# Gate sigmoid, early weight splits and table preloads in the mixing phases of a two-layer kernel

## The chip, the cores and the metric

The kernel runs on one core of a Trainium2 chip. The metric is the device time of one launch in microseconds. TensorE has two clock levels, 1.2 and 2.4 GHz; the profile gives the granted clock as a share of the higher.

## What is computed

Two layers over 1024 prompt rows and 32 sample rows of width 1024, everything in float32. Layer 0 has differential attention, layer 1 stick-breaking attention; both end in an output projection, and behind each stands the same mixing step:

```python
x = x + attention(rmsnorm(x), ...) @ w_out
x = x + sigmoid(x @ ple_w_gate[i]) * (p[i] @ ple_w_proj[i])     # p has 256 columns
# after the last layer
y = rmsnorm(x, final_norm_g)
```

Keys and values of both layers are outputs too. The attention's input projection `rmsnorm(x) @ w_in` has 4096 columns, in 8 groups of 512 (q, k, v: 384, gate: 128).

## The kernel before, in words

Each product of float32 data is made of three matmuls on split operands: a value is rounded to a high part (ACT, a Copy), the rest is the low part (DVE, a subtraction), and the helper `three` at line 107 issues high x high, low x high and high x low. So each matrix is split before it is used, weights too.

The phases stand one behind the other: `lift_phase`, `diff_layer` (names `la_`), `mix_phase` as `mix_a`, `stick_layer` (`lb_`), and `mix_phase` again as `mix_b` with `final_gain`, which makes it the last phase. At the end of a phase all engines meet at a barrier. Each engine has its own program in order, and semaphores tie them; there is no other scheduler.

A mixing phase works feature-major: 8 blocks of 128 output features, and columns (rows of x) in three pieces of 384, 384 and 288. `VISITS` is the order of the work. Visits 0 to 7 are the output projection, one block each. Visits 8 to 15 are gate visits. In `mix_a` each has three units, one a piece. In `mix_b` they have two units (pieces 0 and 1), and visits 16 to 23 go over the blocks again in the reverse order for piece 2, one unit each; there the blocks' weights are loaded and split anew except for the first two. A unit of the gate has 30 matmuls: 6 for p and 24 for x1.

Behind a gate unit stands this chain: DVE bounds the sum (`clamp`, L2049), ACT does Exp (L1930) and Ln with bias 1 (L1932), DVE takes a maximum (`soft`, L2053), ACT does Exp (L1937), DVE multiplies with the p part (`product`, L2058), POOL adds x (`whole` L2113, `add` L2118). In `mix_a` ACT then squares the result (L1948) for the next norm and writes the high part of the next attention's input (L1952), DVE the low part (L2063), POOL sums the squares (L2127), and SP stores the result (L1858) from three buffers, each of which `whole` waits for. TensorE waits for the product of unit v-2 before it starts unit v, since it has two pairs of banks.

The split of the next visit's weights (ACT L1914 and L1916, DVE L2023 and L2025) stands at the head of a visit on both engines, ahead of that visit's units. SP loads a block two visits before its split, once the block's stage half is free.

In `mix_b`'s visits 17 to 22 TensorE also turns a finished tile of 128 rows (`turn`, L2202), ACT forms its statistics (`statistics`: Square L1963, Ln L1967, Exp L1970), DVE scales it (`normed`, L2070) and SP stores it (L1863). The last three tiles come after visit 23.

At the end of `mix_a` ACT and DVE split four of eight blocks of the next attention's first weights (L1999, L2100), TensorE sums the squares over features by a matmul with a constant matrix `mean` (L2226), and once more per token by 18 small matmuls (L2228), and ACT forms the factors of the norm (L2004 to L2010). The token factors are read nowhere later. `stick_layer` then loads and splits blocks 4 to 7 itself (L1119, L1198, L1353), and both halves of the gate's weights (L1202, L1358), while TensorE runs `project` of slots 0 to 5; behind slot 0 it waits for `gw_low` (L1734).

ACT's functions need a table; `preload_act_table_set` names one. It stands in `lift_phase` (L180) for Exp and Ln, and in `stick_layer` (L1324) for Sigmoid. Other table loads are put in by the compiler.

## Time and profile before

| | us |
|---|---|
| median of 3 runs | 1958.19 |
| lowest and highest | 1954.84, 1958.61 |
| the profiled execution | 1955.77 |
| its span, first to last instruction | 1954.0 |
| TensorE busy | 1780.0 (91%) |
| VectorE (DVE) busy | 1023.8 (52%) |
| ScalarE (ACT) busy | 976.7 (50%) |
| GpSimd (POOL) busy | 548.1 (28%) |
| granted clock, mean | 0.972 |

Busy times are shares of one span and overlap each other. `mix_a` runs from about 700 to 959 us, `lb` from 961 to about 1656, `mix_b` to 1954.

### The profile page before, as it was taken

The page shows a single profiled execution, that of the slowest core. Times are in us where ns is not written, and L with a number is a line of the kernel's source. Part 1 is how long each engine was busy: PE and PEld are TensorE (multiplying, and loading weights), DVE is VectorE, ACT ScalarE, POOL GpSimd, SP SyncE. Part 2 cuts the span into 40 slices and gives each one's busy share as a digit, 9 for nine tenths or more (in the row PEclk, how much of TensorE's full clock was granted, in tenths as well). Part 3 has the DMA queues.
Part 4 walks back from the last instruction along what each step waited for, and adds up shares of the span by engine and source line. Part 5 has one row for each costly group of instructions (what it writes and reads, how often), then busy time and mean ns, then how long its engine had stood idle before and what let it go on. Part 6 is the DMA issues. An engine that isn't in the chain of part 4 may idle for free. (4 is left out here: it accounts for less than half of the span.)

```text
span 1954.0 us, 30493 instructions
## 1 busy us (share of the span) xinstructions
PE 1780.0 (91%) x11333; PEld 1580.5 (81%) x11333; DVE 1023.8 (52%) x1821; ACT 976.7 (50%) x2200; POOL 548.1 (28%) x709
## 2 busy tenths in 40 slices
PE   4999999999999989999699999999999997998863
PEld 3878878888788779998598888888888885998863
DVE  5456464564655652256446657565575656434332
ACT  5355454554545542255435445454454545236787
POOL 0131331322313100046314334343343434003310
PEclk9999999999999989999799999999999998999987
DMA  4121111211112043221210212112121122421121
GB/s 155 38 76 47 54 50 40 81 41 54 50 43 81 26 145 98 66 74 52 88 45 23 77 39 61 53 35 77 39 61 42 47 84 73 133 80 44 38 86 57
DMA packets 161507, 124.86 MB, mean 64 GB/s; under 512 B 10960, under 2 KB 152336, under 8 KB 161360
## 3 DMA queue, kind: packets, MB, share of 16 engines
q1 hardware_dynamic: 160496, 122.72, 20.5%
q8 instruction: 91, 1.49, 0.3%
q14 instruction: 56, 0.46, 0.1%
q10 hardware_dynamic: 864, 0.20, 0.0%
HBM read 89.36 MB, written 33.52 MB: 63 GB/s over the span
## 5 line engine op out<-in xcount | busy, mean ns | idle before, releaser
L107 PE MATMUL pj<-h_high,area 128*128 128x384 f32 (+1 forms) x1536 | 380.9, 334 | 17.3 <-issue 5.5
L1517 POOL TENSOR_TENSOR lb_a<-lb_a,lb_remain 128x127 f32<-128x127 f32 (+3 forms) x192 | 237.2, 1255 | 375.1 <-DVE lb_remain L1389 258.6
L107 PE MATMUL pj<-area,h_high 128*128 128x384 f32 (+1 forms) x1152 | 332.1, 351 | 6.7 <-issue 5.5
L107 PEld LDWEIGHTS pj<-h_high,area 128*128 128x128 f32 x1536 | 265.9, 191 | 20.0 <-issue 10.3
L107 PE MATMUL pj<-h_low,area 128*128 128x384 f32 (+1 forms) x768 | 250.5, 326 | 0.0
L1389 DVE TENSOR_TENSOR_SCAN lb_remain<-lb_remain 128x512 f32<-128x512 f32 (+4 forms) x200 | 198.7, 1032 | 67.6 <-ACT lb_remain L1230 66.8
L1230 ACT ACTIVATE lb_remain<-lb_sc 128x512 f32<-128x512 f32 (+4 forms) x200 | 100.1, 501 | 264.5 <-PE lb_sc L1598 234.1
L107 PEld LDWEIGHTS pj<-area,h_high 128*128 128x128 f32 (+1 forms) x1152 | 203.0, 181 | 19.4 <-issue 5.6
L107 PE MATMUL pj<-area,h_low 128*128 128x384 f32 (+1 forms) x576 | 194.7, 338 | 0.0
L107 PEld LDWEIGHTS pj<-h_low,area 128*128 128x128 f32 x768 | 146.3, 191 | 0.0
L455 ACT ACTIVATE la_p<-la_sc,la_nm 128x128 f32<-128x128 f32 (+5 forms) x144 | 105.7, 737 | 33.8 <-DVE la_nm L652 32.9
L757 POOL TENSOR_TENSOR la_ra<-la_tok,cos 128x64 f32<-128x64 f32 (+1 forms) x72 | 23.0, 319 | 335.9 <-ACT la_tok L438 335.9
L1624 PE MATMUL lb_flip<-ident,lb_a 128*128 128x128 f32 (+1 forms) x616 | 94.0, 284 | 22.6 <-POOL lb_a L1517 22.6
L650 DVE TENSOR_REDUCE la_mx<-la_sc 128x1 f32<-128x128 f32 (+5 forms) x144 | 107.6, 747 | 2.2
L107 PEld LDWEIGHTS pj<-area,h_low 128*128 128x128 f32 (+1 forms) x576 | 104.5, 181 | 3.1
L1624 PEld LDWEIGHTS lb_flip<-ident,lb_a 128*128 128x128 f32 (+1 forms) x616 | 64.8, 142 | 50.2 <-POOL lb_a L1517 36.6
L1235 ACT ACTIVATE lb_a<-lb_sc 128x512 f32<-128x512 f32 (+4 forms) x200 | 100.7, 503 | 0.0
L107 PE MATMUL mix_b_g<-mix_b_x_high,area 128*128 128x384 f32 (+1 forms) x384 | 100.5, 349 | 0.0
L1249 ACT ACTIVATE lb_wt<-lb_flip 128x128 f32<-128x128 f32 (+3 forms) x192 | 87.2, 519 | 23.6 <-PE lb_flip L1624 23.6
L107 PE MATMUL mix_a_g<-mix_a_x_high,area 128*128 128x384 f32 (+1 forms) x384 | 91.3, 323 | 0.0
L773 POOL TENSOR_TENSOR area<-stage,area 128x384 fp32r<-128x384 f32 x56 | 64.6, 1181 | 76.1 <-ACT area L427 76.1
L473 ACT ACTIVATE la_wt<-la_third 128x512 f32<-128x512 f32 (+2 forms) x96 | 46.9, 488 | 75.1 <-PE la_third L868 46.5
(305 smaller groups left out, 3988.7 us busy)
## 6 DMA issues: line engine op xcount, KB each, us to landing
stage<-in_a_w_in SPq DMA_DIRECT2D x60, 192.0 KB, 3.3
stage<-in_b_w_in SPq DMA_DIRECT2D x60, 192.0 KB, 3.2
stage<-in_ple_w_gate SPq DMA_DIRECT2D x22, 512.0 KB, 3.7
h_low<-o_t SPq DMA_DIRECT2D x14, 528.0 KB, 6.3
mix_b_xs<-x_mid SPq DMA_DIRECT2D x8, 528.0 KB
lift_xt<-in_x SPq DMA_DIRECT2D x8, 512.0 KB, 4.6
stage<-in_a_w_in SPq DMA_DIRECT2D x16, 256.0 KB, 5.1
out_ak<-la_tok SPq DMA_DIRECT2D x8, 512.0 KB, 3.3
```

The lines of the kernel that those rows point to most:

```text
L107: last = pe.matmul(out, x, y, start=start and n == 0, stop=stop and n == 2, **kw)
L455: act.activation(p[c][u % (3 - c)][0:n, 0:nk], scores_of(u)[:, c, :], ACT.Exp, bias=nm[0:n, u % 2, c:c + 1], accum_out=sums[0:n, u % 2, c: ...
L473: ins = act.activation(wt[:, k0:k0 + nb, off:off + n], bank, ACT.Copy)
L650: dve.reduce_max(mx[0:n, u % 2, c:c + 1], x[:, c, :], AX.X).then_inc(S["dve_link"], 1)
L757: pool.tensor_tensor(xc, x[:, :, 0:16], cos[0:n, t], ALU.mult)
L773: pool.tensor_tensor(w[1][:, k, :], raw_w(k), w[0][:, k, :].bitcast(F32), ALU.subtract).then_inc(S["w_low"], 1)
L1230: act.activation(remain_of(s), scores_of(s), ACT.Sigmoid, scale=-1.0).then_inc(S["keep"], 1)
L1235: act.activation(weights_of(s), scores_of(s), ACT.Sigmoid).then_inc(S["sig"], 1)
L1249: act.activation(wt[hd][:, 4 * c:4 * c + nb, q % 2 * P:(q % 2 + 1) * P], flip[:, hd, 0:width(i)].rearrange("p (b n) -> p b n", n=P), ACT.C ...
L1389: dve.tensor_tensor_scan(out=x, data0=x, data1=x, initial=first, op0=ALU.mult, op1=ALU.min).then_inc(S["scan"], 1)
L1517: pool.tensor_tensor(out, out, after, ALU.mult).then_inc(S["a"], 1)
L1624: last = pe.transpose(flip[0:rows, hd, b // P * n:(b // P + 1) * n], x[:, b:b + rows], ident[0:n, 0:n])
```

## The change

In gate visits below `SECOND` (16), which is all of `mix_a` and the first pass of `mix_b`, the chain is one Sigmoid on ACT and the product. The old chain stays for `mix_b`'s second pass; there the split of the next weights moves between Ln and Exp (ACT) and behind the product (DVE), one visit earlier. Table preloads stand at the start of each mixing phase, at visit 16 of `mix_b`, and ahead of `mix_a`'s last Ln. `mix_a` splits all eight blocks of the next weights: the first four ahead of the last unit's Sigmoid (ACT) and product (DVE), the others behind the last unit, each loaded when a quarter of the stage is free. `stick_layer` no longer loads or splits them, nor waits for `gw_low` behind slot 0. The norm per token goes; `mean` gets memory of its own.

```diff
--- before.py
+++ after.py
@@ -1133,8 +1133,6 @@
...
             load_past(0, Count(table, 0).before("pv"))
-            for k in range(STAGES, KT):
-                load_w(0, k)
             load_gate(0, 1)
@@ -1190,7 +1188,7 @@
...
         def _(act):
-            act.sem_inc(S["w_high"], STAGES)
+            act.sem_inc(S["w_high"], KT)
             start_credits(act, {x: s for x, s in S.items() if x != "w_low"}, 1, 5)
@@ -1317,8 +1315,6 @@
...
 
-            for k in range(STAGES, KT):
-                split_w(0, k)
             for half_ in range(2):
@@ -1332,11 +1328,11 @@
...
         def _(dve):
-            dve.sem_inc(S["w_low"], STAGES + CREDIT)
+            dve.sem_inc(S["w_low"], KT + CREDIT)
             start_credits(dve, {x: s for x, s in S.items() if x != "w_low"}, 2, 5)
...
 
-                dve.sem_inc(S[f"w_loaded{s}"], 16)
+                dve.sem_inc(S[f"w_loaded{s}"], 32)
 
@@ -1488,8 +1484,6 @@
...
 
-            for k in range(STAGES, KT):
-                split_w(0, k)
             for half_ in range(2):
@@ -1730,14 +1724,12 @@
...
                 project(first, x, 1)
-                if x == 0:
-                    pe.wait_ge(S["gw_low"], first.all("gw_low"))
             pe.wait_ge(S["fill"], 1 + 1)
...
 
-def mix_phase(nc, top, name, h, h_offset, stage, area, area_offset, pj, x_in, x_out, p_in, w_out, w_gate, w_proj, ident, norm=None, staged=(),
+def mix_phase(nc, top, name, h, h_offset, stage, area, area_offset, pj, x_in, x_out, p_in, w_out, w_gate, w_proj, ident, norm=None, staged=(), w_next=None,
               final_gain=None):
@@ -1770,6 +1762,9 @@
...
     P_AT = {2 * t + 2: t for t in range(NT + 1)}
+    SECOND = 2 * KT
+    early_splits = [splits_at[i + 1] if i + 1 < len(VISITS) else [] for i in range(len(VISITS))]
+    chained = lambda v: v - sum(len(x) for x in units_at[KT:SECOND])
     SUMS = 3
@@ -1790,14 +1785,13 @@
...
             sq = xs[:, 1, 0:6 * P].rearrange("p (s n) -> p s n", n=3 * P)
-            acc, gain = sb("acc", [P, (NT + 1) * P]), sb("gain", [P, KT])
-            mean = nc.alloc_sbuf_tensor_at(f"{name}_mean", [P, P], F32, offset=area_offset + AREA // 2 * 4)
+            acc, gain, mean = sb("acc", [P, ROWS]), sb("gain", [P, KT]), sb("mean", [P, P])
         eps = sb("eps", [P, 1])
...
                  "sum", "x2", "squared", "acc", "h_high", "h_low", "stored0", "stored1", "stored2", "mean", "mean_log",
-                 "rstd", "gain", "staged", "turned", "square", "normed", "in_high", "fill")
+                 "rstd", "gain", "staged", "turned", "square", "normed", "in_high", "in_low", "fill") + tuple(f"in_loaded{k}" for k in range(STAGES, KT))
         S = {x: nc.alloc_semaphore(f"{name}_{x}") for x in names}
@@ -1898,11 +1892,16 @@
...
                     sp.dma_start(dst, src).then_inc(S["staged"], 16)
+                for k in range(STAGES, KT):
+                    sp.wait_ge(S["in_low"], k - STAGES + 1)
+                    sp.dma_start(raw_in(k - STAGES), w_next[0, k * P:(k + 1) * P, 0:3 * P]).then_inc(S[f"in_loaded{k}"], 16)
                 for v in units_at[-1]:
...
                 sp.wait_ge(S["staged"], 16 * len(staged))
+                for k in range(STAGES, KT):
+                    sp.wait_ge(S[f"in_loaded{k}"], 16)
 
@@ -1924,16 +1923,23 @@
...
 
+            def sigmoid_whole(v):
+
+                act.wait_ge(S["gt"], v + 1)
+                if v >= 2:
+                    act.wait_ge(S["x2"], v - 1)
+                act.activation(sig_of(v), gt_bank(v), ACT.Sigmoid).then_inc(S["sig"], 1)
+
             def sigmoid_log(v):
                 e = sig_of(v)
-                act.wait_ge(S["clamped"], v + 1)
+                act.wait_ge(S["clamped"], chained(v) + 1)
                 act.activation(e, e, ACT.Exp, scale=-1.0).then_inc(S["exp"], 1)
-                act.wait_ge(S["exp"], v + 1)
+                act.wait_ge(S["exp"], chained(v) + 1)
                 act.activation(e, e, ACT.Ln, bias=1.0).then_inc(S["log"], 1)
...
                 e = sig_of(v)
-                act.wait_ge(S["soft"], v + 1)
+                act.wait_ge(S["soft"], chained(v) + 1)
                 act.activation(e, e, ACT.Exp, scale=-1.0).then_inc(S["sig"], 1)
@@ -1950,6 +1956,13 @@
...
                 act.activation(h[0][:, n, cols(c)], x2_of(v), ACT.Copy, scale=gain[:, n:n + 1]).then_inc(S["h_high"], 1)
+
+            def in_high(k):
+                if k < STAGES:
+                    act.wait_ge(S["staged"], 16 * len(staged))
+                else:
+                    act.wait_ge(S[f"in_loaded{k}"], 16)
+                act.activation(w_in[0][:, k, :], raw_in(k % STAGES), ACT.Copy).then_inc(S["in_high"], 1)
 
@@ -1969,9 +1982,13 @@
...
 
+            act.preload_act_table_set("sigmoid_and_others")
             for i, (kind, n, m) in enumerate(VISITS):
-                for j in splits_at[i]:
-                    split_high(j)
+                if i == SECOND:
+                    act.preload_act_table_set("natural_log_exp_and_others")
+                if i < SECOND:
+                    for j in splits_at[i]:
+                        split_high(j)
                 if not final and i == KT:
@@ -1980,8 +1997,17 @@
...
                     else:
-                        sigmoid_log(u)
-                        sigmoid(u)
+                        if not final and u == len(GATE_UNITS) - 1:
+                            act.wait_ge(S["gt"], through(2 * KT - 2))
+                            for k in range(STAGES):
+                                in_high(k)
+                        if i < SECOND:
+                            sigmoid_whole(u)
+                        else:
+                            sigmoid_log(u)
+                            for j in early_splits[i]:
+                                split_high(j)
+                            sigmoid(u)
                         if not final and u > 0:
@@ -1993,28 +2019,23 @@
...
                 next_high(len(GATE_UNITS) - 1)
-                act.wait_ge(S["staged"], 16 * len(staged))
-                act.wait_ge(S["gt"], through(2 * KT - 2))
-                for k in range(STAGES):
-                    act.activation(w_in[0][:, k, :], raw_in(k), ACT.Copy).then_inc(S["in_high"], 1)
+                act.wait_ge(S["gt"], len(GATE_UNITS))
+                for k in range(STAGES, KT):
+                    in_high(k)
+                act.preload_act_table_set("natural_log_exp_and_others")
                 act.wait_ge(S["fill"], 1)
                 act.wait_ge(S["mean"], 1)
-                out, by_token = norm["row"], norm["token"]
+                out = norm["row"]
                 for c in range(NP):
                     act.activation(out[:, cols(c)], yb(c)[:, 0:PIECES[c][1]], ACT.Ln, bias=eps[:, 0:1]).then_inc(S["mean_log"], 1)
-                act.activation(by_token[:, 1, :], yb(3)[:, 0:NT + 1], ACT.Ln, bias=eps[:, 0:1]).then_inc(S["mean_log"], 1)
-                act.wait_ge(S["mean_log"], NP + 1)
-                act.activation(by_token[:, 1, :], by_token[:, 1, :], ACT.Exp, scale=-0.5).then_inc(S["rstd"], 1)
+                act.wait_ge(S["mean_log"], NP)
                 act.activation(out[:, :], out[:, :], ACT.Exp, scale=-0.5)
-                act.wait_ge(S["rstd"], 1)
-                act.activation(by_token[:, 0, :], by_token[:, 1, :], ACT.Copy, scale=DH ** -0.5)
 
...
                 dve.memset(mean[:, :], 1.0 / D)
-                dve.memset(acc[:, ROWS:], 0.0)
             dve.drain().then_inc(S["fill"], 1)
@@ -2049,7 +2070,7 @@
...
             def soft(v):
-                dve.wait_ge(S["log"], v + 1)
+                dve.wait_ge(S["log"], chained(v) + 1)
                 dve.scalar_tensor_tensor(out=sig_of(v), in0=gt_bank(v), scalar=-1.0, in1=sig_of(v), op0=ALU.mult,
@@ -2064,6 +2085,11 @@
...
 
+            def in_low(k):
+                dve.wait_ge(S["in_high"], k + 1)
+                dve.tensor_tensor(w_in[1][:, k, :], raw_in(k % STAGES), w_in[0][:, k, :].bitcast(F32),
+                                  ALU.subtract).then_inc(S["in_low"], 1)
+
             def normed(t):
@@ -2071,8 +2097,9 @@
...
             for i, (kind, n, m) in enumerate(VISITS):
-                for j in splits_at[i]:
-                    split_low(j)
+                if i < SECOND:
+                    for j in splits_at[i]:
+                        split_low(j)
                 if i == KT:
@@ -2083,9 +2110,17 @@
...
                     else:
-                        clamp(u)
-                        soft(u)
-                        product(u)
+                        if not final and u == len(GATE_UNITS) - 1:
+                            for k in range(STAGES):
+                                in_low(k)
+                        if i < SECOND:
+                            product(u)
+                        else:
+                            clamp(u)
+                            soft(u)
+                            product(u)
+                            for j in early_splits[i]:
+                                split_low(j)
                         if not final and u > 0:
@@ -2095,9 +2130,8 @@
...
                 next_low(len(GATE_UNITS) - 1)
-                for k in range(STAGES):
-                    dve.wait_ge(S["in_high"], k + 1)
-                    dve.tensor_tensor(w_in[1][:, k, :], raw_in(k), w_in[0][:, k, :].bitcast(F32), ALU.subtract)
+                for k in range(STAGES, KT):
+                    in_low(k)
 
@@ -2223,10 +2257,7 @@
...
                 for c in range(NP):
-                    pe.matmul(yb(c)[:, 0:PIECES[c][1]], mean[:, :], acc[:, cols(c)], start=True, stop=True)
-                for t in range(NT + 1):
-                    last = pe.matmul(yb(3)[:, t:t + 1], acc[:, t * P:(t + 1) * P], mean[:, 0:1], start=True, stop=True,
-                                     skip_group_check=True)
+                    last = pe.matmul(yb(c)[:, 0:PIECES[c][1]], mean[:, :], acc[:, cols(c)], start=True, stop=True)
                 last.then_inc(S["mean"], 1)
@@ -2269,9 +2300,9 @@
...
             sb = lambda n, s: b.enter_context(nc.sbuf_tensor(n, s, F32))
-            norm = dict(gain=A["b_norm_g"], row=sb("norm_row", [P, ROWS]), token=sb("norm_token", [P, 2, NT + 1]))
+            norm = dict(gain=A["b_norm_g"], row=sb("norm_row", [P, ROWS]))
             mix_phase(nc, top, "mix_a", h, h_offset, stage, area, area_offset, pj, A["x"], x_mid, A["p"][0], A["a_w_out"], A["ple_w_gate"][0],
-                      A["ple_w_proj"][0], ident, norm=norm, staged=first_weights(A["b_w_in"], stage))
+                      A["ple_w_proj"][0], ident, norm=norm, staged=first_weights(A["b_w_in"], stage), w_next=A["b_w_in"])
             stick_layer(nc, top, "lb", h, A["b_w_in"], A["cache_b_k"], A["cache_b_v"], bk, bv, o_dram,
```

## Rows read from the trace of the kernel before

**Rows 1.** Busy time by stretch (us, instructions), granted clock, DMA share, GB/s.
```profile
817.30:943.30 126.00, 118.89 (x722) 115.95 (x721) 70.34 (x106) 63.32 (x128) 65.08 (x64) 1.00 0.21 67
...
1743.80:1854.00 110.20, 96.26 (x513) 93.77 (x511) 43.77 (x63) 76.26 (x96) 36.62 (x31) 0.94 0.15 42
...
1863.00:1930.00 67.00, 39.00 (x220) 37.58 (x220) 23.24 (x35) 54.39 (x77) 9.34 (x12) 0.82 0.24 79
```

**Rows 2.** Waits of TensorE in the three stretches: total us, times, longest.
```profile
PE mix_a_g L107 <- DVE mix_a_sig L2058: 7.1, 7, 1.7
...
PE mix_b_g L107 <- DVE mix_b_sig L2058: 13.9, 8, 3.2
...
PE mix_b_g L107 <- DVE area L2025: 25.9, 6, 6.2
```

**Rows 3.** Table loads of ACT in the groups of the whole span: busy, mean ns.
```profile
L1932 ACT ACT_TABLE_LOAD x24 | 30.8, 1283 | 0.4
...
L1967 ACT ACT_TABLE_LOAD x9 | 11.5, 1283 | 0.2
...
L180 ACT ACT_TABLE_LOAD x1 | 1.3, 1283 | 3.8 <-issue 3.8
```

**Rows 4.** Timeline of mix_a: start, us, engine, line; unit starts, a split, whole.
```profile
822.66 0.52 PE L107 MATMUL mix_a_g<-mix_a_p_high,area 128*128 128x384 f32 x2
...
827.93 0.43 PE L107 MATMUL mix_a_g<-mix_a_p_high,area 128*128 128x288 f32 x2
...
831.90 0.52 PE L107 MATMUL mix_a_g<-mix_a_p_high,area 128*128 128x384 f32 x2
...
883.38 1.05 ACT L1914 ACTIVATE area<-stage 128x1024 fp32r<-128x1024 f32 x1
...
891.78 1.02 POOL L2113 TENSOR_TENSOR mix_a_xs<-mix_a_x_high,mix_a_x_low 128x384 f32<-128x384 f32 x1 [6.49 <-DMA x_mid<-mix_a_xs]
```

**Rows 5.** Timeline of mix_b's second pass, DVE rows and then ACT rows.
```profile
1860.67 1.23 DVE L2023 TENSOR_TENSOR area<-stage,area 128x1024 fp32r<-128x1024 f32 x1 [0.80 <-ACT area L1916]
...
1862.75 0.44 DVE L2049 TENSOR_SCALAR mix_b_sig<-mix_b_g 128x288 f32<-128x288 f32 x1
...
1867.22 0.46 DVE L2058 TENSOR_TENSOR mix_b_sig<-mix_b_g,mix_b_sig 128x288 f32<-128x288 f32 x1 [1.30 <-ACT mix_b_sig L1937]
1871.34 1.28 DVE L2070 SCALAR_TENSOR_TENSOR mix_b_xs<-pj,mix_b_rstd,mix_b_gb 128x1024 f32<-128x1024 f32 x1 [3.67 <-ACT mix_b_rstd L1970]
1872.59 1.23 DVE L2023 TENSOR_TENSOR area<-stage,area 128x1024 fp32r<-128x1024 f32 x1
...
1874.07 0.45 DVE L2049 TENSOR_SCALAR mix_b_sig<-mix_b_g 128x288 f32<-128x288 f32 x1
...
1863.69 1.28 ACT L1932 ACT_TABLE_LOAD   x1
...
1866.74 0.45 ACT L1937 ACTIVATE mix_b_sig<-mix_b_sig 128x288 f32<-128x288 f32 x1
...
1871.21 1.04 ACT L1914 ACTIVATE area<-stage 128x1024 fp32r<-128x1024 f32 x1
```

**Rows 6.** Timeline of mix_b's tail, DVE and ACT.
```profile
1929.18 0.45 DVE L2049 TENSOR_SCALAR mix_b_sig<-mix_b_g 128x288 f32<-128x288 f32 x1
...
1949.61 1.27 DVE L2070 SCALAR_TENSOR_TENSOR stage<-mix_b_g,mix_b_rstd,mix_b_gb 32x1024 f32<-32x1024 f32 x1 [2.83 <-ACT mix_b_rstd L1970]
...
1937.10 1.02 ACT L1963 ACTIVATE mix_b_xs<-pj 128x1024 f32<-128x1024 f32 x1 [3.48 <-PE pj L2202]
```

**Rows 7.** Timeline from the end of mix_a into lb, DVE and PE.
```profile
949.54 2.55 DVE L2100 TENSOR_TENSOR area<-stage,area 128x384 fp32r<-128x384 f32 x4
...
953.95 2.07 PE L2228 MATMUL mix_a_y<-mix_a_mean,mix_a_acc 128*128 128x1 f32 x18
961.51 0.98 PE L107 MATMUL pj<-h_high,area 128*128 128x384 f32 x2 [5.49 <-issue]
...
976.07 0.62 PE L107 MATMUL pj<-h_high,area 128*128 128x384 f32 x2 [2.28 <-DVE lb_wg_low L1358]
```


## The prediction

> **What bounds the kernel now.** I read the page first, for the busy shares and the clock line: TensorE is busy 91% of the span, so only the places where it idles or runs at the lower clock can pay. The stretches show where they are. In the gate part of `mix_a` the tensor engine is 118.9 us busy of 126.0; in the first pass of `mix_b` 96.3 of 110.2; in its second pass 39.0 of 67.0, at granted clock 0.82 [rows 1]. Then the waits of TensorE in these stretches: 7.1 us in 7 waits for the DVE product of the gate in `mix_a`, 13.9 in 8 for the same in `mix_b`'s first pass, 25.9 in 6 for the DVE weight split in the second [rows 2]. Last the groups of ACT: 24 + 24 table loads of 1.28 us at the Ln and the second Exp of the gate (L1932, L1937), 9 + 9 at the norm's Ln and Exp (L1967, L1970), all in `mix_b`, since the list has one load (L180) for all of the attention before `mix_a` [rows 3]. So `mix_b`'s gates are bound by the ACT/DVE chain with its loads, not by matmuls; `mix_a`'s nearly by matmuls.
>
> **The pace that is left.** In `mix_a` a gate unit of 384 columns takes 5.27 us of TensorE without a stall (822.66 to 827.93), one of 288 columns 3.97 (827.93 to 831.90) [rows 4].
>
> **mix_b, first pass.** A unit's ACT work falls from two Exp, a Ln and two loads (2.57 us of loads alone) to one Sigmoid, and DVE's from three instructions to one. By the durations of the steps that it replaces, the new chain from the last matmul to the product's end is about 0.5 + 0.5 us. The split of the next weights stays at the head of each visit: 1.35 us of ACT and 2.1 of DVE [rows 5]. All of it is far below two units of matmuls (10.5 us), so TensorE sets the pace: 16 units x 5.27 = 84.3 us. The pass starts at 1743.8, unit 15 ends at 1828.1 and unit 16 at 1832.1.
>
> **mix_b, second pass.** Before, one visit takes 11.32 us, clamp to clamp (1862.75 to 1874.07) [rows 5]. ACT and DVE do clamp, Exp, load, Ln, soft, load, Exp, product, Square, load, Ln, load, Exp, norm, split, in a ring, while TensorE (3.97 + 1.0 for eight transposes) waits. After: clamp to the slot after Exp 0.94 (1862.75 to 1863.69); Ln 0.47; the split's two ACT instructions, now between Ln and Exp, 1.35 (the slot from 1871.21 holds it) and they cover soft; Exp to product 0.48 (1866.74 to 1867.22). Product is at 3.24 after the clamp and takes 0.46. The low split follows it, then the norm 1.25 (1871.34 to 1872.59), then the next clamp. The low split takes 1.48 with a quiet POOL (1872.59 to 1874.07) and 2.08 with POOL's add beside it (1860.67 to 1862.75) [rows 5]. In the new order POOL's two adds of 0.8 us start just behind the product and lie on the split, so I take 2.08. Meanwhile ACT's Square, Ln and Exp without loads end about 2.0 after the product's start and are covered by the low split. Ring: 3.24 + 0.46 + 2.08 + 1.25 = 7.03 us. Bounds: 6.4 (quiet POOL) and 7.6 (0.6 more for the projection part, as the adds hit both pieces). It is longer than TensorE's 5.0, so this ring is what is late next; DMA has slack, as a block's load is now released a visit earlier.
>
> Clamp of unit 16 at 1832.1, its split ends 5.78 later, so unit 17's clamp is at 1837.9. Five rings to unit 22 give 1873.0; its visit splits nothing, so the next is 5.2 later: clamp of unit 23 at 1878.2. Before it is at 1929.18 [rows 6]. So 51.0 us are gained up to there, 24.9 of them ahead of unit 17's clamp (1862.75) and 26.1 after it.
>
> **mix_b, tail.** Before, from that clamp to the end of the span: 1954.0 - 1929.18 = 24.8 us. Two loads leave the gate chain (2.57). Clamp to the Square of tile 6 is 7.92 now (1929.18 to 1937.10) [rows 6], so 5.35. Three tiles of statistics took 12.5 us from there (Square 1937.10 to norm 1949.61) with six loads; without them ACT needs 4.8, and the transposes at the low clock let it not start tile 8 before 3.4, so 5.1. The norm and the store, 4.4, stay. Sum 14.9, gain 9.9; I take 9.5 for two stores that now come closer together. `mix_b` in all: 60.5.
>
> **mix_a, gate part.** Matmul-bound it is 16 x 5.27 + 8 x 3.97 = 116.1 us against 125.7 from its first to its last matmul: 9.6. What could refuse it is a second ring: split, next load and store issued on SP, the store's landing, POOL's `whole`, the product's add, Square, and the next split. Before, split at 883.38 and `whole` at 891.78, which waited 6.49 for a DMA [rows 4]: 8.4 us; with POOL's three instructions per unit to the second unit's add (5.2) and Square and copy on ACT (0.9) the ring is 14.5, by chance also the matmuls' 14.5. Some 5 us of slack ahead of TensorE lets it drift for the seven visits, so I take 9.5; bounds 4 and 9.6. The preload at the start lies beside the first output matmuls.
>
> **mix_a, end.** The last product comes from Sigmoid, but four low splits of next weights stand before it on DVE (2.55 us [rows 7]). They start behind `next_low` of unit 21, about 1.2 us before the last gate matmul, so the product starts 1.35 after it, where it now starts 3.4 after: 2.0. The 18 small matmuls go, 2.07 [rows 7], and about 0.3 of small ACT steps: sum 4.4. Blocks 4 to 7 of the weights: each low split frees a quarter of the stage, the DMA of 192 KB lands in 3 to 4 us, the last split ends about 6.5 after the last gate matmul, while the mean waits for POOL's two accumulations and three matmuls until 8.8. So 4 x 0.44 us on ACT, 4 x 0.64 on DVE and the 1.28 us load before Ln are covered; without that cover they would cost up to 3. On SP the three last stores stand behind these loads; they land before the row's Exp. I take 4.3, bounds 1 and 4.5.
>
> **lb, start.** Before: project(0) starts 961.51, waits for the four blocks (8 us to split), then for `gw_low`; project(1) starts 976.07 [rows 7]: 14.56 us. After: 12 products at the low clock as in the trace (3.85) and 12 at the full one (2.1), 5.95 us, gain 8.6. Both halves at the low clock would be 7.7: bound 6.9. Behind it DVE still splits both gate halves before the first norm; at about 968.5 on the old scale, before project(2) wants its bank (971.8).
>
> **Sum.** 60.5 + 9.5 + 4.3 + 8.6 = 82.9. The profiled execution took 1955.8 us (span 1954.0), against a median of 1958.2, so it is a quick one of the runs; 1872.9 for its like, 1874 for a median.
>
> **Rules of the Trainium skill.** The loads here take 1.28 us each and the next ACTIVATE follows at once (ring of rows 5: load 1863.69, Exp stage 1.29 later). "ScalarE: Activation LUTs", section "What ACT_TABLE_LOAD costs", puts 2.66 us with a drain on every switch; by it `mix_b`'s visit would gain 5.5 us more, which is more than the visit holds, so the trace's price stands. The same page, "Table sets: the hidden batching unit", names relu, copy, identity and abs as members of every set and does not name square; whether Sigmoid and Square share a set no row shows, and it is the second rival.
>
> **Rivals.**
> (1) Low clock in `mix_b`'s second pass. A stall of 6.2 us is followed by matmuls at half the clock, and TensorE then needs 7.2 + 1.9 us a visit, more than the ring of 7.0. Six visits x 2.1 = 12.6: 1886. For: clock 0.82 in the stretch [rows 1]. Against: the new idle time is only 2 us a visit, and `mix_a` with waits up to 1.7 has clock 1.00 [rows 1]. 12%.
> (2) Square is not in the sigmoid set: in `mix_a` each unit gets two loads on ACT. ACT then needs 3 x (0.53 + 0.43 + 0.55 + 2.57) + 1.4 = 13.6 us a visit, and the ring above grows by 1.3: its 9.5 us are lost, 1883. For: no row has a Square after a Sigmoid. Against: ACT runs Square here without a load of its own behind every Exp, in `mix_a` and in `mix_b`, whose Exp have different loads before them. 10%.
> (3) The change does not do what it says: the loads of `mix_b`'s second pass stay, placed at each Ln and Exp despite the preload. Then four loads x 1.28 x 6 visits and 6 in the tail return, some 35: 1909. Against: L180 is one load for Ln and Exp of all of the first attention [rows 3]. 4%.
> (4) Slower: denser matmuls bring the granted clock down over the whole run. It decides from a mean granted clock under 0.93 (0.97 now, and 83 us of about 1870 are 4.4%); at 0.92, 1975. Against: clock 1.00 where TensorE is busy 118.9 of 126 us [rows 1]. 2%.
> My forecast: 70%; 2% for a gain beyond its bounds, below the range.
>
> **Range.** With the ring at 6.4 and the rest at the good bounds 1868; ring 7.6, `mix_a` 4, its end 1, lb 6.9: 1888. I give 1864 to 1888, which takes in rivals 1 and 2. A difference of 0.2% (4 us) is about what measurement tells from none. Faster 97%, same 1%, slower 2%.
>
> **What would show it.** No loads at Ln or Exp of the gate in `mix_b`, and three or so new single ones in the two phases; product to product 10.5 us a visit in the first pass; clamp to clamp near 7.0 in the second with DVE without idle between product and next clamp; `mix_a` gate at 116 us; no gap in TensorE between the first three projections of `lb`. Wrong would be loads beside Square in `mix_a`, a clamp ring of 9 us with clock below 0.8, or waits for stores in `mix_a` that reach TensorE.

## The result

The changed kernel takes 1870.5 us (median of 4 runs, 1869.84 to 1870.68) against 1958.26 (1954.84 to 1958.61): ratio 0.9555, 95% interval 0.9538 to 0.9572. The forecast was 1874, range 1864 to 1888. The profiled execution took 1870.63 us, its span 1868.8, so 85.2 us of span are gone. TensorE's busy time went from 1780.0 to 1754.2 us (94% of the shorter span), ACT's from 976.7 to 853.8, the mean granted clock from 0.972 to 0.986.

Busy time by stretch in the changed kernel, as in [rows 1]: `mix_a`'s gates, `mix_b`'s first pass, five visits of its second pass (clamp of unit 17 to clamp of unit 22).

```profile
818.90:935.40 116.50, 116.50 (x723) 116.28 (x721) 51.19 (x62) 41.35 (x86) 69.09 (x66) 1.00 0.22 71
1721.20:1809.70 88.50, 88.50 (x514) 88.50 (x513) 27.79 (x33) 18.33 (x32) 38.43 (x33) 1.00 0.18 53
1815.20:1848.50 33.30, 26.78 (x198) 25.59 (x199) 22.72 (x32) 19.88 (x45) 13.61 (x11) 1.00 0.44 143
```

In the first two TensorE is busy for the whole stretch, which before had 7.1 and 13.9 us of waits [rows 2]; now it has none there. What it still waits for from 1721 us on, the second pass and the turn of tile 6:

```profile
PE mix_b_g L107 <- DVE area L2046: 7.2, 6, 1.5
PE pj L2236 <- POOL mix_b_x L2152: 5.8, 1, 5.8
```

ACT's table loads over the whole span, against [rows 3]:

```profile
L1985 ACT ACT_TABLE_LOAD x2 | 2.6, 1283 | 5.1 <-PEq L93 5.1
...
L180 ACT ACT_TABLE_LOAD x1 | 1.3, 1283 | 4.7 <-issue 4.7
L2025 ACT ACT_TABLE_LOAD x1 | 1.3, 1283 | 0.0
L1320 ACT ACT_TABLE_LOAD x1 | 1.3, 1283 | 0.0
L1988 ACT ACT_TABLE_LOAD x1 | 1.3, 1283 | 0.0
```

The 66 loads at Ln and Exp are gone. There are six: one at the head of each mixing phase (L1985), one at visit 16 (L1988), one ahead of `mix_a`'s last Ln (L2025), and the two that were there. None stands beside Square in `mix_a`.

One visit of the second pass, DVE (start, us, engine, line), against [rows 5]:

```profile
1815.17 0.45 DVE L2070 TENSOR_SCALAR mix_b_sig<-mix_b_g 128x288 f32<-128x288 f32 x1
...
1818.19 0.46 DVE L2079 TENSOR_TENSOR mix_b_sig<-mix_b_g,mix_b_sig 128x288 f32<-128x288 f32 x1 [1.13 <-ACT mix_b_sig L1943]
1818.56 1.22 DVE L2044 TENSOR_TENSOR area<-stage,area 128x1024 fp32r<-128x1024 f32 x1
1819.69 1.02 DVE L2046 TENSOR_TENSOR area<-mix_b_raw_proj,area 128x256 fp32r<-128x256 f32 x1
1820.64 1.27 DVE L2096 SCALAR_TENSOR_TENSOR mix_b_xs<-pj,mix_b_rstd,mix_b_gb 128x1024 f32<-128x1024 f32 x1
1821.83 0.44 DVE L2070 TENSOR_SCALAR mix_b_sig<-mix_b_g 128x288 f32<-128x288 f32 x1
```

and ACT in the same visit:

```profile
1815.64 0.44 ACT L1936 ACTIVATE mix_b_sig<-mix_b_sig 128x288 f32<-128x288 f32 x1 [2.96 <-DVE mix_b_sig L2070]
1816.12 0.45 ACT L1938 ACTIVATE mix_b_sig<-mix_b_sig 128x288 f32<-128x288 f32 x1
1816.47 1.04 ACT L1913 ACTIVATE area<-stage 128x1024 fp32r<-128x1024 f32 x1
...
1817.73 0.43 ACT L1943 ACTIVATE mix_b_sig<-mix_b_sig 128x288 f32<-128x288 f32 x1
...
1819.51 0.20 ACT L1983 ACTIVATE mix_b_rstd<-mix_b_ss 128x1 f32<-128x1 f32 x1
```

Clamp to clamp is 6.66 us (1815.17 to 1821.83), where it was 11.32. DVE has no gap between product and next clamp. The low split takes 2.08 us with POOL's adds beside it, and the scale `rstd` (1819.51) is ready before it ends, so the norm waits for nothing.

The end of `mix_a` and the start of `lb`, DVE and then TensorE, against [rows 7]:

```profile
934.03 3.37 DVE L2090 TENSOR_TENSOR area<-stage,area 128x384 fp32r<-128x384 f32 x4
937.33 0.45 DVE L2079 TENSOR_TENSOR mix_a_sig<-mix_a_g,mix_a_sig 128x288 f32<-128x288 f32 x1
...
940.89 1.95 DVE L2090 TENSOR_TENSOR area<-stage,area 128x384 fp32r<-128x384 f32 x4
...
958.54 0.69 DVE L1354 TENSOR_TENSOR lb_wg_low<-stage,lb_wg_high 128x512 fp32r<-128x512 f32 x1 [5.99 <-ACT lb_wg_high L1200]
959.15 0.55 DVE L1364 SCALAR_TENSOR_TENSOR lb_tmp<-pj,norm_row 128x384 f32<-128x384 f32 x1
```

```profile
935.12 0.29 PE L107 MATMUL mix_a_g<-mix_a_x_low,area 128*128 128x288 f32 x1
940.79 2.90 PE L2260 MATMUL pj<-mix_a_acc,mix_a_mean 128*128 128x384 f32 x4 [5.39 <-POOL mix_a_acc L2161]
...
949.85 0.98 PE L107 MATMUL pj<-h_high,area 128*128 128x384 f32 x2 [5.19 <-issue]
...
952.87 0.65 PE L107 MATMUL pj<-h_high,area 128*128 128x384 f32 x2
...
955.63 0.51 PE L107 MATMUL pj<-h_high,area 128*128 128x384 f32 x2
...
959.85 0.52 PE L107 MATMUL pj<-h_high,area 128*128 128x384 f32 x2
```

The reader sees the first four low splits end just before the last product (937.33, 1.9 us after the last gate matmul ends at 935.4), the last four start at 940.89, the mean at 940.79 without small matmuls behind it, and in `lb` 24 matmuls of slot 0, 24 of slot 1 and slot 2 in one row (949.85, 955.63, 959.85).

The span in parts, each from its marks in the two traces (first and last matmul of the gates, first of `lb`'s slots 0 and 1, first gate matmul of `mix_b`, clamps of units 16, 17, 22 and 23):

| part | before | after | gain | forecast |
|---|---|---|---|---|
| up to `mix_a`'s first gate matmul | 817.4 | 819.0 | -1.6 | 0 |
| `mix_a` gates | 125.9 | 116.4 | 9.5 | 9.5 |
| to `lb`'s first matmul | 18.2 | 14.4 | 3.8 | 4.3 |
| slot 0 to slot 1 | 14.6 | 5.8 | 8.8 | 8.6 |
| to `mix_b`'s first gate matmul | 767.9 | 765.6 | 2.3 | 0 |
| `mix_b` first pass, to clamp 16 | 111.0 | 88.5 | 22.5 | |
| clamp 16 to 17 | 7.8 | 5.5 | 2.3 | 24.9 with the row above |
| clamp 17 to 23 | 66.4 | 38.4 | 28.0 | 26.1 |
| clamp 23 to the end | 24.8 | 15.2 | 9.6 | 9.5 |

The two parts with no forecast of their own hold nothing that the change touches between their marks, bar the table load at the head of each mixing phase; over the twelve profiled executions of this study the first lies between 815.0 and 819.2 and the second between 765.0 and 770.6, so -1.6 and 2.3 are within what an execution varies.

### The profile page after: what moved, and what is told of

Read it like the earlier page. It is cut to its first block and busy times, and to the rows that moved or that the text cites. A ratio compares the mean times of both kernels' runs of the same rounds, so it can differ in the third digit from the quotient of the medians.

```text
span 1868.8 us, 30233 instructions
## 1 busy us (share of the span) xinstructions
PE 1754.2 (94%) x11315; PEld 1561.5 (84%) x11315; DVE 987.7 (53%) x1740; ACT 853.8 (46%) x2054; POOL 555.6 (30%) x709
## 5 line engine op out<-in xcount | busy, mean ns | idle before, releaser
L107 PE MATMUL mix_b_g<-mix_b_x_high,area 128*128 128x384 f32 (+1 forms) x384 | 91.6, 324 | 0.0
L633 DVE TENSOR_TENSOR la_qk_low<-pj,la_qk_high 128x256 fp32r<-128x256 f32 (+1 forms) x72 | 28.9, 402 | 103.3 <-ACT la_qk_high L442 103.3
```

Source lines behind the costliest of these rows:

```text
L107: last = pe.matmul(out, x, y, start=start and n == 0, stop=stop and n == 2, **kw)
L633: dve.tensor_tensor(qk[1][:, :, cols], turned_bank(t), qk[0][:, :, cols].bitcast(F32), ALU.subtract).then_inc(S["turned_low"], 1)
```

## Experiments

Each was timed beside the kernel before. The marks are those of the table above. Six runs take one part back or do one part alone (e1 to e6); e7 and e8 try what the trace shows as next, e9 both of them, and e10 is the changed kernel once more.

**e1: the preload alone.** The kernel before with one line.

```diff
+            act.preload_act_table_set("natural_log_exp_and_others")
             for i, (kind, n, m) in enumerate(VISITS):
```

> The kernel before, with one table preload (Ln and Exp together) ahead of the visits of each mixing phase and nothing else. My theory: most of the gain of the change is the 66 table loads of mix_b, so this alone brings about 60 of the 88 us: first pass of mix_b at the pace of its matmuls (about 86 us, not 110), clamp to clamp in the second pass 6.2 to 6.7 us (not 11.3), tail 8 us shorter; time about 1898. Rival: the shorter chain (Sigmoid) and the moved splits carry the gain, and the loads were mostly beside other work: then at most 35 us, 1923 or more.

Measured: 1896.4 us (1895.4 to 1897.7), ratio 0.969 (0.9676 to 0.9705). `mix_b` from its first gate matmul to the end is 148.1 us, in the changed kernel 147.6, before 210.0. ACT has four table loads left: the two of before at L180 and L1324, and one at the head of each mixing phase.

```profile
L1972 ACT ACT_TABLE_LOAD x2 | 2.6, 1283 | 5.1 <-PEq L93 5.1
```

The first pass to clamp 16 takes 88.6 us, in the changed kernel 88.5; I had expected about 86. The tail is 9.7 us shorter, where I had 8. DVE in the second pass, two clamps with product and norm between them:

```profile
1846.51 0.45 DVE L2050 TENSOR_SCALAR mix_b_sig<-mix_b_g 128x288 f32<-128x288 f32 x1
...
1848.92 0.46 DVE L2059 TENSOR_TENSOR mix_b_sig<-mix_b_g,mix_b_sig 128x288 f32<-128x288 f32 x1 [0.51 <-ACT mix_b_sig L1937]
1850.49 1.28 DVE L2071 SCALAR_TENSOR_TENSOR mix_b_xs<-mix_b_y,mix_b_rstd,mix_b_gb 128x1024 f32<-128x1024 f32 x1 [1.11 <-ACT mix_b_rstd L1970]
...
1853.22 0.45 DVE L2050 TENSOR_SCALAR mix_b_sig<-mix_b_g 128x288 f32<-128x288 f32 x1
```

Clamp to clamp 6.71 us. So 61.9 of the 62.4 us that `mix_b` gained are the loads. The rest of the gain is `mix_a` and `lb`: `mix_a`'s gates stay at 125.5 here. The rival falls: neither Sigmoid nor the moved split is needed for it.

**e2: no preload at visit 16.**

```diff
-                if i == SECOND:
-                    act.preload_act_table_set("natural_log_exp_and_others")
```

> The changed kernel without the preload at visit 16 of mix_b. My theory: the compiler then puts a load at each Ln and each Exp behind it, four in a visit; clamp to clamp goes from 6.66 to about 11.1 us, the tail gets 7.7 us longer, time about 1909. Rival (the compiler keeps one set for the whole stretch once it meets Ln): one load, time within 2 us of the changed kernel's 1870.5.

Measured: 1909.95 us, ratio 0.9765 (0.9747 to 0.9782). The loads are back, one at each Ln and each Exp behind it: 9 at L1980 and 9 at L1983 for the norm, 8 at L1938 and 8 at L1943 for the gate.

```profile
L1980 ACT ACT_TABLE_LOAD x9 | 11.5, 1283 | 0.2
```

```profile
1838.79 0.45 DVE L2068 TENSOR_SCALAR mix_b_sig<-mix_b_g 128x288 f32<-128x288 f32 x1
...
1848.64 1.28 DVE L2094 SCALAR_TENSOR_TENSOR mix_b_xs<-pj,mix_b_rstd,mix_b_gb 128x1024 f32<-128x1024 f32 x1 [1.61 <-ACT mix_b_rstd L1983]
1849.84 0.45 DVE L2068 TENSOR_SCALAR mix_b_sig<-mix_b_g 128x288 f32<-128x288 f32 x1
```

Clamp to clamp is 11.05, and the norm waits 1.61 us for `rstd`, which it does not do in the changed kernel in a visit that has a low split. The tail is 24.8 us, and `mix_b` is 186.5 us, 38.9 more than in the changed kernel: 1.14 us for each of the 34 loads, less than the 1.28 that a load itself takes, since some of it lies beside other work (in a visit beside the low split, which in the changed kernel ends 0.9 us after `rstd` is ready). This is the case of the prediction's third rival. My own rival, one load for the whole stretch, falls.

**e3: the splits of the second pass back at the head of a visit.**

```diff
-                if i < SECOND:
-                    for j in splits_at[i]:
-                        split_high(j)
+                for j in splits_at[i]:
+                    split_high(j)
...
-                            for j in early_splits[i]:
-                                split_high(j)
```

and the same on DVE.

> The changed kernel with the weight splits of mix_b's second pass back at the head of the next visit on ACT and DVE; preloads and Sigmoid kept. My theory: DVE's sum is the same and its low split then meets a quiet POOL (1.5 us, not 2.1), so clamp to clamp stays at 6.2 to 7.0 and the time within 3 us of 1870.5: moving the split brought little. Rival: the early split is what shortens the ring, by 1 us or more a visit: 1877 or more.

Measured: 1873.7 us (1872.9 to 1875.0), ratio 0.9574 (0.956 to 0.9589), so 3.2 above the changed kernel's first runs, a little more than the 3 I allowed, and not clear of them by the intervals. DVE:

```profile
1837.09 0.45 DVE L2067 TENSOR_SCALAR mix_b_sig<-mix_b_g 128x288 f32<-128x288 f32 x1
...
1841.06 1.28 DVE L2093 SCALAR_TENSOR_TENSOR mix_b_xs<-mix_b_y,mix_b_rstd,mix_b_gb 128x1024 f32<-128x1024 f32 x1 [1.11 <-ACT mix_b_rstd L1983]
1842.32 1.23 DVE L2041 TENSOR_TENSOR area<-stage,area 128x1024 fp32r<-128x1024 f32 x1
...
1843.79 0.45 DVE L2067 TENSOR_SCALAR mix_b_sig<-mix_b_g 128x288 f32<-128x288 f32 x1
```

Clamp to clamp 6.70. The low split now takes 1.47 us (1842.32 to 1843.79), but the norm waits 1.11 for `rstd` ahead of it. From the clamp to the product it is 2.40 us, not 3.02, as ACT's split no longer stands in that chain. `mix_b` is 148.3 us, 0.7 more than in the changed kernel; the other 1.5 us of span difference lie in phases that the edit does not touch. Moving the split paid 0.7 us, hardly any of it in the ring: it took the wait of 1.11 us out and put 0.62 into the chain and 0.61 into a low split that now runs beside POOL.

**e4: the old chain in `mix_a`.**

```diff
-                        if i < SECOND:
-                            sigmoid_whole(u)
+                        if final and i < SECOND:
+                            sigmoid_whole(u)
...
-                        if i < SECOND:
-                            product(u)
+                        if final and i < SECOND:
+                            product(u)
```

with the two preloads of `mix_a` left out.

> The changed kernel with the old chain (clamp, Exp, Ln, maximum, Exp, product) in mix_a only, under the Ln and Exp table. My theory: mix_a's gate part goes back from 116.2 to about 125.7 us and its end gets 1 to 3 us longer, since the chain of the last unit stands behind four low splits; time 1880 to 1884. Rival: matmuls waited there for stores, not for the chain: gate part stays below 119 us and the time below 1875.

Measured: 1885.1 us (1883.4 to 1888.1), ratio 0.9634 (0.9618 to 0.9649), a little above what I expected. The gates take 125.5 us, 9.1 more, so it was the chain and not the stores that the matmuls waited for, and from the last gate matmul to `lb` it is 19.4, not 14.4: 5.0 more, where I had 1 to 3. DVE at that place:

```profile
943.47 3.35 DVE L2090 TENSOR_TENSOR area<-stage,area 128x384 fp32r<-128x384 f32 x4
946.74 0.45 DVE L2070 TENSOR_SCALAR mix_a_sig<-mix_a_g 128x288 f32<-128x288 f32 x1
...
949.14 0.46 DVE L2079 TENSOR_TENSOR mix_a_sig<-mix_a_g,mix_a_sig 128x288 f32<-128x288 f32 x1 [0.51 <-ACT mix_a_sig L1943]
```

The clamp itself stands behind the four low splits (3.35 us with POOL beside them), so the whole chain of 2.4 us starts only then. So Sigmoid is worth 14 us in `mix_a` with the splits in their new place, and in `mix_b` at most the 0.5 us between e1 and the changed kernel.

**e5: blocks 4 to 7 of `lb`'s weights split in `lb`.** Undone: `in_high` and `in_low` for `k >= STAGES`, their loads on SP, and the credits in `lb`; there, as before:

```diff
+            for k in range(STAGES, KT):
+                load_w(0, k)
             load_gate(0, 1)
...
+            for k in range(STAGES, KT):
+                split_w(0, k)
             for half_ in range(2):
                 split_gate(0, half_)
```

> The changed kernel with blocks 4 to 7 of lb's first weights loaded and split at lb's start again, without the wait for gw_low. My theory: the end of mix_a doesn't get shorter (the four splits lie there beside the mean's wait), and project(1) of lb starts 11 to 12 us after project(0), not 5.8, so the time is 1876 to 1878. Rival: the early loads cost at mix_a's end what they save in lb: within 2 us of 1870.5.

Measured: 1877.5 us (1876.0 to 1878.0), ratio 0.9592 (0.9577 to 0.9606). The end of `mix_a` is as long (14.5 us), so the added splits there were covered, and slot 1 starts 11.5 us after slot 0: the early loads save 5.7 us in `lb` and cost nothing before it. TensorE's two waits at the start:

```profile
947.42 0.98 PE L107 MATMUL pj<-h_high,area 128*128 128x384 f32 x2 [5.22 <-issue]
954.84 1.01 PE L107 MATMUL pj<-h_high,area 128*128 128x384 f32 x2 [3.60 <-DVE area L1353]
```

Behind the wait of 3.60 us the matmuls run at the low clock again (1.01 us for two, 0.52 at the high one), as they did behind the first.

**e6: the wait for `gw_low` restored.**

```diff
                 project(first, x, 1)
+                if x == 0:
+                    pe.wait_ge(S["gw_low"], first.all("gw_low"))
```

> The changed kernel with TensorE's wait for both halves of the gate's weights behind slot 0 of lb, as before. My theory: the second half's low split ends 9.3 us after project(0) starts, so project(1) starts 3.7 us later than now; time 1874 to 1875. Rival: project(2) had to wait for the same DVE stretch anyway, so nothing is lost: within 1 us of 1870.5.

Measured: 1874.1 us (1871.8 to 1877.0), ratio 0.9576 (0.956 to 0.9592). Alone this does not stand clear of the changed kernel. The trace does:

```profile
948.80 0.98 PE L107 MATMUL pj<-h_high,area 128*128 128x384 f32 x2 [5.16 <-issue]
957.49 0.62 PE L107 MATMUL pj<-h_high,area 128*128 128x384 f32 x2 [1.82 <-DVE lb_wg_low L1354]
```

Slot 1 starts 8.7 us after slot 0, 2.9 later than in the changed kernel, not 3.7, as the gate half landed sooner here. In the changed kernel, slot 2 starts at 959.85 and the norm that frees its bank ends at 959.70: taking the wait away left 0.15 us of room before the next one.

**e7: the next clamp ahead of the norm**, in `mix_b`'s second pass on DVE.

```diff
                         else:
-                            clamp(u)
+                            if i == SECOND:
+                                clamp(u)
                             soft(u)
                             product(u)
                             for j in early_splits[i]:
                                 split_low(j)
+                            if u + 1 < len(GATE_UNITS):
+                                clamp(u + 1)
```

> The changed kernel with DVE's clamp of the next unit ahead of the tile's scaling in mix_b's second pass. My theory: the ring through ACT and DVE sets the pace there, so the 1.19 us of scaling leave it: clamp to clamp 5.5 us, not 6.66, and 6 to 7 us in all, 1864. Rival: the stores and block loads or TensorE itself hold the pace once it is asked to be below 6.5: clamp to clamp 6.2 or more and 1868 or more.

Measured: 1863.6 us (1862.7 to 1865.6), ratio 0.952 (0.9504 to 0.9536). `mix_b` is 140.8 us, 6.8 less than in the changed kernel. DVE, and TensorE's waits in these visits:

```profile
1833.35 0.44 DVE L2070 TENSOR_SCALAR mix_b_sig<-mix_b_g 128x288 f32<-128x288 f32 x1
1833.71 1.27 DVE L2096 SCALAR_TENSOR_TENSOR mix_b_xs<-pj,mix_b_rstd,mix_b_gb 128x1024 f32<-128x1024 f32 x1
...
1837.87 1.02 DVE L2046 TENSOR_TENSOR area<-mix_b_raw_proj,area 128x256 fp32r<-128x256 f32 x1
1838.82 0.45 DVE L2070 TENSOR_SCALAR mix_b_sig<-mix_b_g 128x288 f32<-128x288 f32 x1
...
PE mix_b_g L107 <- DVE area L2046: 2.5, 6, 0.8
```

Clamp to clamp is 5.47 us: ACT's Exp and Ln now run beside the norm's 1.2. TensorE waits 2.5 us in six visits; its own 5.0 us a visit are nearly the pace.

**e8: the first four next-weight splits one unit earlier in `mix_a`.**

```diff
-                        if not final and u == len(GATE_UNITS) - 1:
+                        if not final and u == len(GATE_UNITS) - 2:
```

on ACT and on DVE.

> The changed kernel with mix_a's first four next-weight splits ahead of the last unit but one, on ACT and DVE, where both idle 3.5 to 4 us. My theory: the last product starts 0.4 us after the last gate matmul, not 1.9, and everything behind it to lb's start moves by 1.5 to 1.9 us, 1869. Rival: the last four blocks' splits or the table load are next in line and eat it: lb's start moves by less than 0.5.

Measured: 1869.35 us (1867.8 to 1869.9), ratio 0.955 (0.9536 to 0.9564), which the time alone does not tell from the changed kernel.

```profile
927.79 2.89 DVE L2090 TENSOR_TENSOR area<-stage,area 128x384 fp32r<-128x384 f32 x4 [0.42 <-ACT area L1965]
...
934.52 0.46 DVE L2079 TENSOR_TENSOR mix_a_sig<-mix_a_g,mix_a_sig 128x288 f32<-128x288 f32 x1 [1.78 <-ACT mix_a_sig L1931]
...
947.15 0.98 PE L107 MATMUL pj<-h_high,area 128*128 128x384 f32 x2 [5.16 <-issue]
```

The last product starts 0.44 us after ACT's last Sigmoid (934.08) and no longer behind the splits. `lb` starts 13.1 us after the last gate matmul, not 14.4: 1.3, a little under my 1.5. Slot 0 took 6.4 us there, not 5.8, as the clock rose 4.6 us after its start and not 3.0, so half of it is not seen in the span.

**e9 and e10: both edits, beside the changed kernel on the same chip.**

> The changed kernel with both edits of e7_clamp_ahead and e8_split_a_unit_earlier. My theory: they lie in different phases, so their gains add: 7 + 1.5 us below the changed kernel of the same call, 1862. Rival: an order elsewhere gives back the smaller one: less than 7.5 us below it.

> The changed kernel itself, once more, on the chip of e9_both: 1870 to 1871 us; what it differs from its first runs is how far runs on another chip differ.

Measured: 1862.7 us (1860.6 to 1864.2), ratio 0.9513 (0.9501 to 0.9526), against 1870.9 (1868.8 to 1872.3), ratio 0.9556 (0.9543 to 0.9569). 8.2 us less; 8.5 was expected, and the rival's bound of 7.5 lies within the spread of the two, so that the gains add in full is not shown by the times. By the marks `mix_b` is 141.0 (147.5) and the step to `lb` 13.3 (14.4). It has the lowest median of all versions, 0.9 us below e7, whose runs overlap with it.

## Why the prediction held, step by step

**What bounds it.** Right. `mix_b` was bound by ACT's chain with its loads: e1 took them out, e2 put them back in, and both times came out within 2 us of what was expected. The price of 1.28 us is that of the load itself (the one at 1863.69 in [rows 5] is followed 1.29 us later by the Ln, which the prediction calls the Exp stage). What a load adds to a ring is less where part of it lies beside other work: 1.15 us each from before to e1 (11.32 to 6.71 for four), 1.10 from the changed kernel to e2.

**First pass of `mix_b`, `mix_a` gates.** Right: 88.5 us to unit 16's clamp against 88.3 worked out, and 116.4 against 116.1. The ring of splits, stores and POOL, which could have refused the gain in `mix_a`, never reached TensorE, whose wait list for that stretch is empty.

**The ring of the second pass.** The mechanism was right, its size 0.37 us too long: 6.66, not 7.03. The split was priced right (2.08). Three slots were shorter: the product's 0.37 before the split, not 0.46; the norm's 1.19, not 1.25; clamp to product 3.02, not 3.24, as two of ACT's instructions that do not wait for each other overlap a little (Ln to split 0.35, not 0.47). Five rings make the 1.9 us by which `mix_b` gained more.

**The tail.** 9.6 against 9.5, and partly by luck. The working came to 9.9 and gave 0.4 back for stores that come closer together; the stores cost nothing (last norm to the end is 4.4 us before and after). What was too large is the 2.57 us for the gate's two loads: clamp to Square took 5.85 us, not 5.35, since the second load had run beside DVE's maximum, for which ACT waits 0.53 us without it.

**`lb`'s start.** 8.8 against 8.6. The clock rose 3 us after slot 0 began (952.87), sooner than the 3.85 taken. In the eight executions with `lb`'s start as in the changed kernel slot 0 took 5.78 to 7.07 us, by when the clock rose, so the profiled one is the quickest. That no wait followed was close: the working had DVE done 3.3 us before slot 2 wants its bank (968.5 and 971.8 on the old scale), and its norm ended 0.15 us before, as the second gate half landed only 8.0 us after slot 0 began (ACT's split of it starts at 957.88).

**The end of `mix_a`.** 0.5 less than forecast. The four low splits took 3.37 us, not 2.55. Neither is the time of four splits alone, which is 1.95 (940.89): in the row of before the first of the four lay beside one of POOL's sums and took 1.14 us instead of 0.55, in the changed kernel the first two lay beside POOL (1.37 and 1.14). So the last product came 0.6 us later than forecast, and the small matmuls gave back 1.7 us, not 2.07 (from the mean's start to TensorE's last matmul of the phase it was 5.61 us and is 3.87); 0.3 us between product and mean made up for a third of this. No run puts the small matmuls back alone, so their share is read from the two traces only. The cover named for the last four splits was there (e5).

**What each part is worth.** Here the prediction was not wrong in its sum but loose in its words. It named Sigmoid, the preloads and the moved splits together as what makes `mix_b`'s pace. The one line of e1 does it. Had I worked out the old chain without loads (13.96 - 4 x 1.28 = 8.8 us a visit, under TensorE's 10.5) the sum would have said so.

**Rivals.** Low clock in the second pass: 1.00 in the stretch, rejected. Square outside the sigmoid set: no loads in `mix_a`, rejected; the Trainium skill ("ScalarE: Activation LUTs", "Table sets: the hidden batching unit") leaves square out of its list of members of every set, and this trace adds it for this one. The loads stay: rejected for the changed kernel. Where e2 makes it so, 1909.95 us stand against the rival's 1909, and that is luck: its 24 and 6 loads at 1.28 us are 38.4 us, not "some 35", which would have made 1912; e2 has 34 such loads, they cost 38.9 us in `mix_b`, and the kernel that they are added to was 3.5 us quicker than forecast. Denser matmuls, lower clock: the mean rose to 0.986.

**The total and the range.** By the marks 85.2 us were gained and 82.9 forecast: 1.9 of the difference is the ring, 0.6 the two stretches that the change does not touch, and the rest nearly cancels. The median came 3.5 us below 1874, since the forecast also took the profiled execution of before as 1.1 us quicker for its kind than a median, and that of the changed kernel was at its median. The low end was misadded: a ring of 6.4 and every other term at its good bound give about 1870, not 1868.

## What to carry to other kernels

Read the list of table loads before anything else on ACT: here a preload of one set that holds both Ln and Exp was worth 62 us (e1) and the rewriting around it 26. Then sum the ring that a visit goes round on each engine, instruction by instruction, and look for the one that can stand behind the signal for the next round; moving it (e7) took 1.2 us off each visit without making anything faster. A wait that is removed pays only until the next one binds, which the trace shows (2.9 us gained in e6's place, 0.15 us of room left behind it), and a step moved from one wait into another place of the same ring (the split in e3) is worth next to nothing, however sensible it looks.

## What the runs showed that I had not expected

Small DVE splits (128 x 384, four in a row) took 1.95 us alone, 2.55 to 3.37 us with POOL at work: one beside an instruction of POOL took 1.14 to 1.37 us, not 0.55. It goes the other way too: POOL's add of 128 x 288 took 0.80 us in a quiet stretch (e3) and 1.64 beside DVE's low split of 128 x 1024, which took its usual 1.22. The projection's low split of 128 x 256 took 0.42 us in a quiet stretch and 1.01 to 1.23 beside POOL's adds.

In `lb` one stretch of unchanged code (slot 1 to the end of the output projection) took 765.0 to 770.6 us in twelve profiled executions, so differences of 3 us between two kernels can't be put down to an edit by their times alone; the marks around the edit can.
